# Eight small loads on ScalarE's queue, gate weights in halves, Pool's large memsets behind the first norm

## Chip, cores and metric

The kernel runs on one core of a Trainium2 chip. The time is device microseconds from the launch to the end on that core, as the median of several executions. The names of the engines are TensorE (PE in the profile, with its weight loads as PEld), VectorE (DVE), ScalarE (ACT), Pool (GpSimd) and SP (the engine that only issues transfers here).

## The reference

One decoder layer on 1024 tokens of width 1024, in float32. Cut to what matters:

```
h = x + W_out . concat(RMSNorm(StickBreakingAttention(q, k, v)), ConformerConv(c))
        with [q | k | v | c] = RMSNorm(x) . W_in          W_in: 1024 x 2560
y = h + PEER(RMSNorm(h))
PEER: per token 8 heads, each finds its 16 best of 16384 experts by two small key tables,
      act = gelu(u_tab[expert] . h),  y += gate * act * v_tab[expert]
```

The attention has 8 heads of 64 and is causal; the convolution group is a gated linear unit (`a * sigmoid(gate)`), a causal depthwise convolution of 31 taps, a layer norm and a swish. The expert rows (128 per token, from two tables of 64 MB) are gathered from device memory.

## The kernel before

The 1024 tokens are eight chunks of 128, one token per partition. `phase0` does norm, projection and, for the first chunk, everything else up to the list of experts; `phase1` gathers and adds expert rows for all chunks while it runs the front part of the next chunk beside it. This case touches only the begin of `phase0`.

For each chunk, ScalarE squares x (`square_x`, L664) and takes the root of the mean, VectorE scales (`norm_x`, L845 is the wide multiplication into `xn`), TensorE transposes `xn` (`transpose_x`, L492), ScalarE copies the result to `xnT` with the gains of the norm (`copy_xT`, L679), and TensorE multiplies by `w_in` in five banks of 512 columns (`project`, L514). The banks are A and G (the two halves of the gated linear unit), then Q, K, V, and lie in `w_sb`, 2 MB each. A float32 product of 128 x 512 appears as two records, so a bank is 16 records and a chunk 80.

The order on each queue is written out by hand, and semaphores join the queues:

- SP (L367 on) issues x of the first chunk, then the eight small vectors: five into `rows`, one partition per 128 numbers (L374), two head gains doubled by a broadcast (L377), and `conv_w` into `taps_row`, 31 partitions of 2 KB (L380). All eight add to one semaphore, `small_in`. Then it loads the banks of `w_in` (`load_w`, L386), the first bank A in two halves with a semaphore each, the others whole, with the x of the second chunk behind Q.
- Pool (L445 on) makes the identity and the mask, then fills `kT` and `vals` (each 128 x 4096) and the halo of `conv_in` with zeros (L458 to L460) and is then idle until the first list of experts.
- TensorE first waits for the identity and for all of `small_in`, and turns `rows` and `taps_row` (L474, L476). Only then come x's transposes and the projections.
- VectorE copies what was turned out of PSUM into `vec` and `taps` (L959, L960). `copy_xT` waits for both copies, since it needs the gains.
- ScalarE begins with a table load for the square root (L799), then `square_x(0)`.

The zeros are waited for by ScalarE only: before its first writes into `conv_in` (L730), `kT` (L719) and `vals` (L707).

Of the kernel before, what the change touches and what calls it, by code (L numbers as in the profile page):

```python
# [22 lines left out]
P = 128  # L23
SEQ, D = 1024, 1024
CHUNKS = SEQ // P
KT_D = D // P
HEADS, HD = 8, 64
AW = HEADS * HD
CW = D - AW
AB = AW // P  # L30
CB = CW // P
# [261 lines left out]
def phase0(block, nc, S, base, psum, ident, ident_b, mask, kT, vals, keys_T, w_kept, wo_sb, wq_sb, actT, qT,  # L293
# [5 lines left out]
    Q, K, V, A, G = range(GROUPS)  # L299
    ORDER = (A, G, Q, K, V)  # L300
# [10 lines left out]
    rows = m.tile("rows", [P, P], F32)  # L311
    taps_turn = Map(nc, m.at)
    taps_row = m.tile("taps_row", [TAPS, CW], F32)
# [22 lines left out]
    sem = nc.alloc_semaphore  # L336
# [13 lines left out]
    gated, glu_done = sem("gated"), sem("glu_done")  # L350
    qT_stored, hT_stored, h_kept = sem("qT_stored"), sem("hT_stored"), sem("h_kept")
    S.kT_copied, S.qT_stored, S.hT_stored = kT_copied, qT_stored, hT_stored
    w_second = sem("w_second")
    keys_in, keys_turned, keys_copied = sem("keys_in"), sem("keys_turned"), sem("keys_copied")
    NSMALL = 8
    LAST = CHUNKS - 1
# [10 lines left out]
    @block.sync  # L367
    def _(sp):
        sp.dma_start(x_in[:, :], x[0, 0:P, :]).then_inc(x_loaded, 16)

        r = 0
        for v, n in ((norm_mix_g, KT_D), (attn_out_g, AB), (conv_b, CB), (conv_ln_g, CB),
                     (conv_ln_b, CB)):
            sp.dma_start(rows[r:r + n, :], v[0, :].rearrange("(n p) -> n p", p=P)).then_inc(small_in, 16)  # L374
            r += n
        for v in (q_norm_g, k_norm_g):
            sp.dma_start(rows[r:r + 1, :].rearrange("o (two d) -> o two d", two=2),  # L377
                         v[0:1, :].unsqueeze(1).to_broadcast([1, 2, HD])).then_inc(small_in, 16)
            r += 1
        sp.dma_start(taps_row[:, :], conv_w[0, :, :]).then_inc(small_in, 16)  # L380
        def load_w(g):

            parts = 2 if g == ORDER[0] else 1
            for n in range(parts):
                k, rows_in = KT_D // parts, D // parts
                sp.dma_start(w_sb[:, ORDER.index(g), n * k:(n + 1) * k, :],  # L386
                             w_in[0, n * rows_in:(n + 1) * rows_in, g * BANK:(g + 1) * BANK]
                             .rearrange("(k p) n -> p k n", p=P)).then_inc(w_second if n else w_loaded[g], 16)

        def next_x(i):  # L390
            sp.wait_ge(x_normed, i + 1)
            sp.dma_start(x_in[:, :], x[0, bass.ds((i + 1) * P, P), :]).then_inc(x_loaded, 16)

        def store_q(i):
            sp.wait_ge(qT_copied, i + 1)
            sp.dma_start(qT_spill[bass.ds(i, 1), :, :].rearrange("o p n -> (o p) n"),
                         qT_out[:, :]).then_inc(qT_stored, 16)

        def store_h(i):
            sp.wait_ge(hT_copied, i + 1)  # L400
            sp.dma_start(hT_spill[:, :, bass.ds(i * P + HALO, P)], hT_out[:, :, :]).then_inc(hT_stored, 16)

        for g in (A, G, Q):
            load_w(g)
        next_x(0)
        for g in (K, V):
            load_w(g)
        for n, k in enumerate((peer_k1, peer_k2)):
            sp.dma_start(keys[:, :, n, :], k[0].rearrange("h n d -> n h d")).then_inc(keys_in, 16)
        store_h(0)  # L410
        sp.dma_start(w_kept[:, :, :], w_out[0].rearrange("(k p) n -> p k n", p=P)).then_inc(S.wo_loaded, 16)
        next_x(1)
        store_q(0)
        store_h(1)
        next_x(2)
        sp.wait_ge(keys_turned, 1)
        sp.dma_start(S.g_ffn[:, :], norm_ffn_g[0:1, :].to_broadcast([P, D])).then_inc(S.g_loaded, 16)
        sp.wait_ge(S.attended, HEADS)
        sp.dma_start(S.h_res[:, :], x[0, 0:P, :]).then_inc(S.x_in, 16)
        sp.wait_ge(S.tapped, TAPS * CB)  # L420
        sp.wait_ge(hT_stored, 32)
        sp.dma_start(conv_in[:, :, :], hT_spill[:, :, P:2 * P + HALO]).then_inc(S.c_in, 16)
        store_q(1)
        sp.wait_ge(qT_stored, 32)
        sp.dma_start(qT[:, :, :].rearrange("p b t -> p (b t)"), qT_spill[1]).then_inc(S.q_in, 16)
        sp.wait_ge(S.mixed, 1)
        for n, landed in enumerate((S.wq_first, S.wq_loaded)):
            at = slice(n * BANK, (n + 1) * BANK)
            sp.dma_start(w_kept[:, :, at], peer_wq[0, :, at].rearrange("(k p) n -> p k n", p=P)).then_inc(landed, 16)
        for i in range(2, CHUNKS):  # L430
            store_h(i)
            if i < LAST - 1:
                next_x(i + 1)
            if i == LAST:
                sp.wait_ge(projected[G], CHUNKS)
                sp.dma_start(wo_sb[:, :, :], w_out[0].rearrange("(k p) n -> p k n", p=P)).then_inc(S.wo_loaded, 16)
            store_q(i)
        sp.wait_ge(projected[K], CHUNKS)
        sp.dma_start(wq_sb[:, :, :], peer_wq[0].rearrange("(k p) n -> p k n", p=P)).then_inc(S.wq_loaded, 16)
        sp.wait_ge(qT_stored, 16 * CHUNKS)  # L440
        sp.wait_ge(hT_stored, 16 * CHUNKS)

    @block.gpsimd
    def _(pool):
        nc.gpsimd.memset(ident[:, :], 0.0).then_inc(zeroed, 1)  # L445
        nc.gpsimd.memset(mask[:, :], 0.0).then_inc(zeroed, 1)
        pool.wait_ge(zeroed, 2)
        nc.gpsimd.affine_select(out=ident[:, :], in_=ident[:, :], compare_op=ALU.not_equal, fill=1.0,
                                base=0, pattern=[[-1, P]], channel_multiplier=1).then_inc(consts, 1)

        nc.gpsimd.affine_select(out=mask[:, :], in_=mask[:, :], compare_op=ALU.is_gt, fill=NEG,
                                base=0, pattern=[[-1, P]], channel_multiplier=1).then_inc(consts, 1)
        nc.gpsimd.iota(counting[:, :, :], pattern=[[1, TOPK], [0, PH]], base=0, channel_multiplier=0,
                       allow_small_or_imprecise_dtypes=True).then_inc(consts, 1)
        pool.wait_ge(consts, 3)
        nc.gpsimd.tensor_copy(ident_b[:, :], ident[:, :]).then_inc(consts, 1)

        nc.gpsimd.memset(kT[:, :, :], 0.0).then_inc(zeroed, 1)  # L458
        nc.gpsimd.memset(vals[:, :, :], 0.0).then_inc(zeroed, 1)
        nc.gpsimd.memset(conv_in[:, :, 0:HALO], 0.0).then_inc(zeroed, 1)  # L460

        pool.wait_ge(S.experts_done, 1)
        for e in range(EARLY):
            if e >= EARLY_RING:
                pool.wait_ge(S.dotted, e - EARLY_RING + 1)
            nc.gpsimd.indirect_dma_start(  # L466
                w_kept[:, e % EARLY_RING, :], None, peer_u[0],
                bass.IndirectOffsetOnAxis(S.experts[0][:, e:e + 1], 0)).then_inc(S.early_in[e % EARLY_RING], 16)

    @block.tensor  # L470
    def _(pe):
# [25 lines left out]
        def project(i, g, half=None):  # L497
            if i == 0 and half != 1:
                pe.wait_ge(w_loaded[g], 16)
            if half != 1:  # L500

                if g == V:
                    pe.wait_ge(glu_done, i + 1)
                elif g == K:
                    pe.wait_ge(gated, i + 1)
                elif i:
                    pe.wait_ge(*{A: (v_copied, i), G: (kT_copied, i), Q: (qT_copied, i)}[g])
            n = KT_D // 2
            for k in {None: range(KT_D), 0: range(n), 1: range(n, KT_D)}[half]:
                if i == 0 and g == ORDER[0] and k == n:  # L510
                    pe.wait_ge(w_second, 16)
                if g == ORDER[0]:
                    pe.wait_ge(xT_copied, KT_D * i + k + 1)
                last = nc.tensor.matmul(ps[g], xnT[:, k, :], w_sb[:, ORDER.index(g), k, :],  # L514
                                        start=k == 0, stop=k == KT_D - 1)
            if half != 0:
                last.then_inc(projected[g], 1)
# [140 lines left out]
    def _(act):  # L658
# [119 lines left out]
        def chunk(i):  # L778
            if 3 <= i < LAST:
                square_x(i + 1)  # L780
                root_x(i + 1)
            gate(i)
            if i == 0:
                copy_glu(0)
                square_x(1)
                root_x(1)
            square_qk(i)
            root_qk(i)
            if i == 0:
                copy_qk(0)  # L790
            else:
                copy_glu(i)
            copy_v(i)
            if i < LAST:
                copy_xT(i + 1)
            if i:
                copy_qk(i)

        nc.scalar.preload_act_table(ACT.Sqrt)  # L799
        square_x(0)  # L800
# [1282 lines left out]
```

## Time and profile before

| | |
|---|---|
| runs | 2910.17, 2914.2 and 2912.07 us |
| median | 2912.07 us |
| span of the profiled execution, first to last instruction | 2910.3 us |
| another time of the profiled execution | none is given |
| TensorE busy | 89% of the span |
| VectorE, Pool, ScalarE busy | 73%, 68%, 30% |
| moved by DMA | 1125.04 MB, 387 GB/s on average |
| mean granted TensorE clock | 0.994 |

Times in the rows are microseconds from the begin of the span. In a timeline row stand the start, the duration, the engine, the line and what is written from what; a bracket at its end tells how long the engine had been idle and what ended that. A row of windows gives the stretch and its length, then busy time (and instructions) of PE, PEld, DVE, ACT and POOL, and last the granted clock, the busy share of the DMA engines and GB/s. "Q" behind an engine's name is its issuing of transfers. "Landing" is the time from the issue of a transfer until its semaphore has its full value. Busy shares are averages over stages with different limits, so a stretch has to be looked at by itself.

### The profile page before, as it was taken

What the parts mean: (1) busy time and instruction counts of PE and PEld (TensorE: products, weight loads), DVE (VectorE), ACT (ScalarE), POOL (GpSimd) and SP (SyncE); (2) the same over time, 40 slices, a digit from 0 to 9 for tenths busy, and PEclk for the clock granted to TensorE, in tenths of its full rate; (3) what the DMA queues carried; (4) which work ended last, traced back from release to release, by engine and by line L of the source; (5) the groups of instructions that cost most, each with busy time, mean ns of one, the idle gap of its engine ahead of it and who ended that gap; (6) DMA issues with size and microseconds to landing.
All of it is one profiled execution on the core that took longest, in us unless ns stands there. A gap on an engine that the chain in (4) does not pass through costs nothing.

```text
span 2910.3 us, 29785 instructions
## 1 busy us (share of the span) xinstructions
PE 2591.2 (89%) x7585; PEld 1173.6 (40%) x7585; DVE 2110.6 (73%) x5267; ACT 871.6 (30%) x2022; POOL 1986.1 (68%) x2061
## 2 busy tenths in 40 slices
PE   8999979889978899799979999799988999777777
PEld 4544434433523444244523444244523445222222
DVE  5789758866887678777887778777787757744444
ACT  3223232243213421253214521264214631211111
POOL 1026566677777777777777777777777777777775
PEclk9999999999999999999999999999999999999999
DMA  6239899899999999999999999999999999999999
GB/s 239 96 127 382 331 416 369 316 402 414 419 419 419 413 419 419 409 414 409 416 416 406 411 419 419 419 392 413 419 419 399 385 419 419 415 420 419 420 419 364
DMA packets 321344, 1125.04 MB, mean 387 GB/s; under 512 B 35937, under 2 KB 43641, under 8 KB 321176
## 3 DMA queue, kind: packets, MB, share of 16 engines
q0 software_dynamic: 294912, 1073.87, 91.7%
q1 hardware_dynamic: 26264, 49.27, 4.8%
q8 instruction: 63, 1.03, 0.1%
q14 instruction: 105, 0.86, 0.1%
HBM read 1114.62 MB, written 8.39 MB: 386 GB/s over the span
## 4 chain that ended last, share of the span: by engine, by line
PE 41%; DMA 25%; issue 16%; POOL 12%; DVE 4%; ACT 2%; POOLq 0%; SPq 0%; ACTq 0%; DVEq 0%
PE psum L1614 21%; DMA w_kept<-in_peer_u,experts 12%; DMA ring_v<-in_peer_v,experts 10%; PE psum L514 9%; POOL w_kept L1517 7%; POOL ring_v L1517 5%; PE psum L1038 3%; PE psum L1064 3%; PE psum L1548 2%; DVE w_kept L1933 1%; PE psum L1574 1%; DMA w_kept<-in_peer_v,experts 1%; PE psum L1564 1%; DMA qT_spill<-qT_out 1%; ACT L1751 0%
## 5 line engine op out<-in xcount | busy, mean ns | idle before, releaser
L1614 PE MATMUL psum<-ring_v,diag 128*128 128x512 f32 x3364 | 1619.6, 607 | 252.6 <-DMA ring_v<-in_peer_v,experts 163.9
L1933 DVE CUSTOM_DVE_ANT_0 w_kept<-w_kept,psum 128x1024 f32<-128x1024 f32 x928 | 1125.5, 1217 | 551.2 <-DMA w_kept<-in_peer_u,experts 548.1
L1517 POOL DMA_INDIRECT w_kept<-in_peer_u,experts x928 | 898.2, 968 | 300.1 <-issue 231.4
L1517 POOL DMA_INDIRECT ring_v<-in_peer_v,experts x878 | 847.8, 966 | 327.3 <-issue 234.5
L1614 PEld LDWEIGHTS psum<-ring_v,diag 128*128 128x128 f32 x3364 | 587.1, 191 | 1058.8 <-issue 775.2
L1760 ACT ACTIVATE diag<-ident,weights 128x128 f32<-128x128 f32 x981 | 354.2, 393 | 746.9 <-PE psum L1614 589.9
L1614 PE MATMUL psum<-w_kept,diag 128*128 128x512 f32 x560 | 269.9, 604 | 37.3 <-DMA w_kept<-in_peer_v,experts 23.5
L514 PE MATMUL psum<-w_sb,xnT 128*128 128x512 f32 x640 | 283.5, 599 | 0.8 <-ACT xnT L679 0.8
L466 POOL DMA_INDIRECT w_kept<-in_peer_u,experts x96 | 90.2, 940 | 236.7 <-DVE experts L1324 184.9
L1889 DVE SCALAR_TENSOR_TENSOR acc<-conv_in,taps,acc 128x128 f32<-128x128 f32 x720 | 205.0, 346 | 0.2
L514 PEld LDWEIGHTS psum<-w_sb,xnT 128*128 128x128 f32 x640 | 120.6, 192 | 143.4 <-issue 137.7
L1517 POOL DMA_INDIRECT w_kept<-in_peer_v,experts x146 | 141.2, 967 | 47.6 <-issue 39.0
L1614 PEld LDWEIGHTS psum<-w_kept,diag 128*128 128x128 f32 x560 | 97.1, 190 | 170.2 <-issue 155.2
L1064 PEld LDWEIGHTS psum<-actT,wq_sb 128*128 128x128 f32 x896 | 118.8, 191 | 57.0 <-issue 56.9
L1858 DVE TENSOR_TENSOR_SCAN log_keep<-log_keep,relu_z 128x256 f32<-128x256 f32 (+3 forms) x88 | 90.4, 1027 | 59.9 <-ACT log_keep L1693 59.7
L1064 PE MATMUL psum<-actT,wq_sb 128*128 128x128 f32 x896 | 119.5, 275 | 0.0
L1708 ACT ACTIVATE actT<-psum 128x256 f32<-128x256 f32 (+3 forms) x88 | 44.9, 510 | 242.8 <-PE psum L1564 242.8
L1038 PE MATMUL psum<-wo_sb,actT 128*128 128x512 f32 x224 | 113.2, 592 | 0.0
L952 DVE CUSTOM_DVE_ANT_0 w_kept<-w_kept,psum 128x1024 f32<-128x1024 f32 x96 | 110.5, 1215 | 0.3 <-DMA w_kept<-in_peer_u,experts 0.3
L1751 ACT ACTIVATE geld<-dots 128x16 f32<-128x16 f32 x64 | 13.3, 214 | 303.3 <-DVE dots L1933 303.0
L1548 PE MATMUL psum<-kT,qT 64*128 64x512 f32 (+3 forms) x176 | 84.0, 557 | 2.1 <-DVE relu_z L1860 1.1
L1574 PEld LDWEIGHTS psum<-vals,actT 128*128 128x128 f32 x560 | 71.7, 192 | 27.2 <-issue 26.8
(230 smaller groups left out, 1750.9 us busy)
## 6 DMA issues: line engine op xcount, KB each, us to landing
w_kept<-in_peer_u,experts POOLq DMA_INDIRECT x1024, 9.5
ring_v<-in_peer_v,experts POOLq DMA_INDIRECT x878, 9.5
w_sb<-in_w_in SPq DMA_DIRECT2D x4, 2048.0 KB, 17.6
x_in<-in_x SPq DMA_DIRECT2D x8, 512.0 KB, 6.3
w_kept<-in_w_out SPq DMA_DIRECT2D x1, 4096.0 KB, 14.8
h_res<-in_x SPq DMA_DIRECT2D x8, 512.0 KB, 6.8
w_kept<-in_peer_wq SPq DMA_DIRECT2D x2, 2048.0 KB, 10.6
wo_sb<-in_w_out SPq DMA_DIRECT2D x1, 4096.0 KB, 19.9
```

The costliest lines, as they stand in the source:

```text
L514: last = nc.tensor.matmul(ps[g], xnT[:, k, :], w_sb[:, ORDER.index(g), k, :], start=k == 0, stop=k == KT_D - 1)
L952: nc.vector.tensor_tensor_reduce(out=row, in0=row, in1=hn, scale=1.0, scalar=0.0, op0=ALU.mult, op1=ALU.add, accum_out=S.dots[:, e:e + 1]) ...
L1038: product = nc.tensor.matmul(z[0][:, j * BANK:(j + 1) * BANK], S.actT[:, k, :], wo_sb[:, k, j * BANK:(j + 1) * BANK], start=k == 0, stop=k ...
L1064: product = nc.tensor.matmul(z[0][:, h * P:(h + 1) * P], wq_sb[:, k, h * P:(h + 1) * P], S.actT[:, k, :], start=k == 0, stop=k == KT_D - 1)
L1517: nc.gpsimd.indirect_dma_start(slot(kind, n), None, peer_u[0] if kind == "u" else peer_v[0], bass.IndirectOffsetOnAxis(S.experts[c % 2][:, ...
L1548: last = nc.tensor.matmul(z, qT[lo:lo + HD, a // 2, :], kT[lo:lo + HD, a // 2, lo_key:hi_key], start=True, stop=not has_own)
L1574: last = nc.tensor.matmul(o_ps[:, a * HD:(a + 1) * HD], S.attT[:, b, :], vals[:, b, a * HD:(a + 1) * HD], start=n == 0, stop=n == len(orde ...
L1614: last = nc.tensor.matmul(y_ps[:, j * BANK:(j + 1) * BANK], diag[:, e % DIAGS, :], slot("v", n)[:, j * BANK:(j + 1) * BANK], start=e == 0, ...
L1760: nc.scalar.activation(diag[:, e % DIAGS, :], ident[:, :], ACT.Copy, scale=weights[:, e:e + 1]).then_inc(diagonal, 1)
L1858: nc.vector.tensor_tensor_scan(l[:, back], l[:, back], r[:, back], carry, ALU.add, ALU.add).then_inc(S.summed, counts(f))
L1889: nc.vector.scalar_tensor_tensor(out=acc[:, c, :], in0=conv_in[:, c, t:t + P], scalar=taps[:, c, t:t + 1], in1=acc[:, c, :], op0=ALU.mult, ...
L1933: nc.vector.tensor_tensor_reduce(out=row, in0=row, in1=hn, scale=1.0, scalar=0.0, op0=ALU.mult, op1=ALU.add, accum_out=dots[:, e:e + 1]).t ...
```

## The change

Three edits. ScalarE issues the eight small loads, ahead of its table load, so that SP goes from x straight to the weights. The bank G is loaded in two halves as A is, each with a semaphore, and TensorE waits for the second half in the middle of the bank. Pool waits for the first norm (`x_normed`) before it fills `kT`, `vals` and the halo.

```diff
--- before.py
+++ after.py
@@ -350,7 +350,8 @@
     gated, glu_done = sem("gated"), sem("glu_done")
     qT_stored, hT_stored, h_kept = sem("qT_stored"), sem("hT_stored"), sem("h_kept")
     S.kT_copied, S.qT_stored, S.hT_stored = kT_copied, qT_stored, hT_stored
-    w_second = sem("w_second")
+    HALVED = (A, G)
+    w_second = {g: sem(f"w_second{g}") for g in HALVED}
     keys_in, keys_turned, keys_copied = sem("keys_in"), sem("keys_turned"), sem("keys_copied")
     NSMALL = 8
     LAST = CHUNKS - 1
@@ -368,24 +369,14 @@
     def _(sp):
         sp.dma_start(x_in[:, :], x[0, 0:P, :]).then_inc(x_loaded, 16)
 
-        r = 0
-        for v, n in ((norm_mix_g, KT_D), (attn_out_g, AB), (conv_b, CB), (conv_ln_g, CB),
-                     (conv_ln_b, CB)):
-            sp.dma_start(rows[r:r + n, :], v[0, :].rearrange("(n p) -> n p", p=P)).then_inc(small_in, 16)
-            r += n
-        for v in (q_norm_g, k_norm_g):
-            sp.dma_start(rows[r:r + 1, :].rearrange("o (two d) -> o two d", two=2),
-                         v[0:1, :].unsqueeze(1).to_broadcast([1, 2, HD])).then_inc(small_in, 16)
-            r += 1
-        sp.dma_start(taps_row[:, :], conv_w[0, :, :]).then_inc(small_in, 16)
         def load_w(g):
 
-            parts = 2 if g == ORDER[0] else 1
+            parts = 2 if g in HALVED else 1
             for n in range(parts):
                 k, rows_in = KT_D // parts, D // parts
                 sp.dma_start(w_sb[:, ORDER.index(g), n * k:(n + 1) * k, :],
                              w_in[0, n * rows_in:(n + 1) * rows_in, g * BANK:(g + 1) * BANK]
-                             .rearrange("(k p) n -> p k n", p=P)).then_inc(w_second if n else w_loaded[g], 16)
+                             .rearrange("(k p) n -> p k n", p=P)).then_inc(w_second[g] if n else w_loaded[g], 16)
 
         def next_x(i):
             sp.wait_ge(x_normed, i + 1)
@@ -455,6 +446,7 @@
         pool.wait_ge(consts, 3)
         nc.gpsimd.tensor_copy(ident_b[:, :], ident[:, :]).then_inc(consts, 1)
 
+        pool.wait_ge(x_normed, 1)
         nc.gpsimd.memset(kT[:, :, :], 0.0).then_inc(zeroed, 1)
         nc.gpsimd.memset(vals[:, :, :], 0.0).then_inc(zeroed, 1)
         nc.gpsimd.memset(conv_in[:, :, 0:HALO], 0.0).then_inc(zeroed, 1)
@@ -507,8 +499,8 @@
                     pe.wait_ge(*{A: (v_copied, i), G: (kT_copied, i), Q: (qT_copied, i)}[g])
             n = KT_D // 2
             for k in {None: range(KT_D), 0: range(n), 1: range(n, KT_D)}[half]:
-                if i == 0 and g == ORDER[0] and k == n:
-                    pe.wait_ge(w_second, 16)
+                if i == 0 and g in HALVED and k == n:
+                    pe.wait_ge(w_second[g], 16)
                 if g == ORDER[0]:
                     pe.wait_ge(xT_copied, KT_D * i + k + 1)
                 last = nc.tensor.matmul(ps[g], xnT[:, k, :], w_sb[:, ORDER.index(g), k, :],
@@ -795,6 +787,17 @@
                 copy_xT(i + 1)
             if i:
                 copy_qk(i)
+
+        r = 0
+        for v, n in ((norm_mix_g, KT_D), (attn_out_g, AB), (conv_b, CB), (conv_ln_g, CB),
+                     (conv_ln_b, CB)):
+            act.dma_start(rows[r:r + n, :], v[0, :].rearrange("(n p) -> n p", p=P)).then_inc(small_in, 16)
+            r += n
+        for v in (q_norm_g, k_norm_g):
+            act.dma_start(rows[r:r + 1, :].rearrange("o (two d) -> o two d", two=2),
+                         v[0:1, :].unsqueeze(1).to_broadcast([1, 2, HD])).then_inc(small_in, 16)
+            r += 1
+        act.dma_start(taps_row[:, :], conv_w[0, :, :]).then_inc(small_in, 16)
 
         nc.scalar.preload_act_table(ACT.Sqrt)
         square_x(0)
```

## Rows read from the trace of the kernel before

**Rows 1.** Windows, long stretches: busy us per engine, granted clock, DMA share, GB/s
```profile
100.00:350.00 250.00, 248.50 (x788) 124.89 (x787) 214.57 (x588) 68.08 (x134) 93.05 (x99) 1.00 0.66 246
...
400.00:2900.00 2500.00, 2218.32 (x6433) 987.23 (x6432) 1814.72 (x4466) 748.05 (x1773) 1859.39 (x1924) 1.00 1.02 409
```

**Rows 2.** Timeline, SP's DMA issues at the begin: start us, us, what
```profile
1.20 0.37 SPq L374 DMA_DIRECT2D rows<-in_norm_mix_g  x1
...
2.92 0.73 SPq L377 DMA_DIRECT2D rows<-in_q_norm_g  x1
3.69 0.57 SPq L377 DMA_DIRECT2D rows<-in_k_norm_g  x1
4.31 0.41 SPq L380 DMA_DIRECT2D taps_row<-in_conv_w  x1
4.77 0.41 SPq L386 DMA_DIRECT2D w_sb<-in_w_in  x1
5.22 0.50 SPq L386 DMA_DIRECT2D w_sb<-in_w_in  x1
5.76 0.83 SPq L386 DMA_DIRECT2D w_sb<-in_w_in  x1
6.63 5.20 SPq L386 DMA_DIRECT2D w_sb<-in_w_in  x1
```

**Rows 3.** Timeline, ScalarE, VectorE and Pool in the first chunk: start us, us
```profile
0.74 1.28 ACT L799 ACT_TABLE_LOAD   x1 [0.74 <-PEq L2073]
...
4.10 1.06 ACT L664 ACTIVATE xn<-x_in 128x1024 f32<-128x1024 f32 x1 [2.08 <-DMA x_in<-in_x]
...
5.90 4.21 DVE L845 TENSOR_SCALAR xn<-x_in,x_stat 128x1024 f32<-128x1024 f32 x1
...
5.92 3.51 POOL L459 MEMSET vals<- 128x4096 f32 x1
...
11.01 0.18 DVE L959 COPY vec<-psum 128x26 f32<-128x26 f32 x1 [0.89 <-PE psum L476]
...
32.56 0.59 ACT L730 ACTIVATE conv_in<-psum 128x512 f32<-128x512 f32 x1
...
35.93 0.75 DVE L845 TENSOR_SCALAR xn<-x_in,x_stat 128x1024 f32<-128x1024 f32 x1
```

**Rows 4.** Chain of waits from the begin: start us, us, what
```profile
4.31 5.82 DMA taps_row<-in_conv_w
...
10.97 1.90 PE psum L492 x8
12.87 18.72 PE psum L514 x40
```

**Rows 5.** Timeline, TensorE's weight loads of the first projections
```profile
12.67 0.50 PEld L514 LDWEIGHTS psum<-w_sb,xnT 128*128 128x128 f32 x2 [0.20 <-DMA w_sb<-in_w_in]
...
20.80 0.19 PEld L514 LDWEIGHTS psum<-w_sb,xnT 128*128 128x128 f32 x1 [0.35 <-DMA w_sb<-in_w_in]
```

**Rows 6.** Tile w_sb, issues at 4.77, 5.76 and 6.63: time to landing
```profile
DMA to landing us min/median/max: 7.9/7.9/7.9
...
DMA to landing us min/median/max: 15.0/15.0/15.0
...
DMA to landing us min/median/max: 19.5/19.5/19.5
```

**Rows 7.** Windows, the first 21 us (columns as in rows 1)
```profile
1.00:4.00 3.00, 0.00 (x0) 0.00 (x0) 0.00 (x0) 1.02 (x1) 2.69 (x6) 1.00 0.51 179
4.00:5.00 1.00, 0.00 (x0) 0.00 (x0) 0.00 (x0) 0.90 (x1) 1.00 (x1) 1.00 0.00 1
5.00:6.00 1.00, 0.00 (x0) 0.00 (x0) 0.41 (x3) 0.45 (x3) 1.00 (x2) 1.00 0.26 21
6.00:10.00 4.00, 0.00 (x0) 0.00 (x0) 4.00 (x1) 0.00 (x0) 3.57 (x2) 1.00 0.97 302
12.70:20.80 8.10, 8.10 (x17) 3.58 (x16) 0.00 (x0) 2.88 (x8) 0.00 (x0) 1.00 1.05 387
```

## The prediction, made before the change was run

> **What bounds the kernel now.** I read the stretches of the whole span first, then the first 40 us in detail, since all three edits lie there. In the long stretch from 400 us on, the DMA engines are busy all the time [rows 1]: this is the gather of expert rows, and its length does not depend on how the kernel began. Before it, from 100 to 350 us, TensorE is busy 248.5 of 250 us [rows 1]. So a microsecond won or lost at the begin is handed on through a busy TensorE and then through a busy DMA, one for one, if it reaches TensorE's first projection at all. Nothing in these two stretches can multiply it. The question is thus when the first projection starts, and whether weights keep up with it afterwards.
>
> The begin, in the order of the chain of waits: SP issues x, then the eight small loads from 1.20 to 4.72, then weights [rows 2]. The chain goes from the last small issue, the convolution taps, over 5.82 us until they land at 10.13, then TensorE, which goes on without a break of weight until 31.59 [rows 4]. Beside it stands a second path that is ready at the same time: ScalarE squares x at 4.10, and VectorE's norm takes 5.90 to 10.11, 4.21 us for an operation that takes 0.75 us for the next chunk [rows 3]. Pool's memset of `vals` lies over it, 5.92 to 9.43 [rows 3]; 9.43 plus 0.75 is 10.18, so VectorE seems to have waited for the memset and then worked. A third path: the first half of A's weights lands at 4.77 + 7.9 = 12.67, exactly when the first projection's weight load begins, and that one waited 0.20 for it [rows 5, 6]. G's weights land at 5.76 + 15.0 = 20.76, and TensorE's first load of them is at 20.80 after a wait for that DMA [rows 5, 6]. So three things end within a few tenths of each other, and a gain needs all three to go.
>
> **The change, part by part.**
>
> *Pool.* The two large memsets and the halo move behind the first norm. That frees the norm: it costs 0.75 and not 4.21, 3.46 us. The memsets then run for 3.51 + 3.51 + 0.20 us from the norm's end (8.1, below) to about 15.3. Their first user is ScalarE's copy into `conv_in` at 32.56 [rows 3], 17 us later; without that cover it would cost the whole 7.2. What VectorE does meanwhile are the two copies of the small vectors out of PSUM at 11.0 [rows 3]; see the fourth case.
>
> *The small loads on ScalarE's queue.* I charge ScalarE what SP's issues took: 3.52 us, from 0.74 to 4.26, with the taps issued from 3.85 on and not from 4.31, 0.46 us earlier. Behind them on ScalarE stand its table load (1.28 [rows 3], until now hidden before x landed) and the square: it starts at 5.54 and not 4.10. The norm started 1.80 after the square did [rows 3], so now at 7.34, and ends at 8.09. That is 2.0 us earlier than now, although ScalarE is 1.4 us later. SP's weights start to be issued at 1.20, 3.57 us earlier. But x's 0.5 MB fills the DMA engines until about 4.0 (179 GB/s from 1 to 4), and weights moved only from about 6 on [rows 7], so the stream of weights wins some 2.2 us: A's first half 10.5 or sooner, no longer behind the taps, G's last byte 18.6, Q's 6.63 + 19.5 = 26.1 [rows 2, 6] becomes 23.9. TensorE takes 24 records from 20.80 to 31.59, or 7.2 us for 16, one bank of weights; a bank of 2 MB lands in 5.4 us at 387 GB/s [rows 4, 5, 7], so beyond Q weights never bind.
>
> *What the taps now meet.* The stream from 6 to 10 us is 302 GB/s, 1.21 MB [rows 7], enough for the taps and A's first half (1.11 MB); yet that half lands 2.54 us after the taps. A sixteenth of it, 65 KB, takes 2.7 us at 387/16 = 24 GB/s: one of the 16 DMA engines carries all 62 KB of the taps, and its share of A waits behind them. In the change the taps sit on another queue, and that engine has weights queued first (A and G issued from 1.20 to 3.1). Bounds for the landing of the taps: if they pass at once, 3.85 + 1.5 + 2.6 = 8.0 (1.5 for the first byte: issued at 4.31, nothing moves from 4 to 5 and little from 5 to 6 [rows 7]); if everything takes as long as now, 3.85 + 5.82 = 9.67; if in addition every packet of theirs waits for one of weights, 2.6 more, 12.3. Between 8.0 and 12.3 I take the middle, 10.15, which is where it stands now: the 0.46 us of earlier issue is eaten by sharing. The Trainium skill says in "DMA: Bandwidth & Descriptors", Queues, rings and completion order, that a DMA engine takes turns between its queues packet by packet; by that the upper half, 9.67 to 12.3, is the likely one, and the sum would be up to 2 us worse than mine. No row here shows two such queues at work.
>
> *G in halves.* One more issue on SP (0.4 us, hidden behind a full queue), one more wait on TensorE. G's first load waited 0.35, where its neighbours wait 0.24 for nothing but their turn; 0.1 us goes.
>
> *Sum.* Taps 0.0; the wait for A's first half −0.2; the wait for G −0.1; all else hidden. That is −0.3 us. The profiled execution spans 2910.3 us and gives no other time of its own; the median of the runs is 2912.07, 1.8 us above it, and I take that difference as it is: 2911.8.
>
> **The rivals.** A difference under 0.2% (5.8 us) is about what a measurement of this kernel cannot tell from no change.
>
> *The taps pass at once.* Landing at 8.0, x's transposes would start 0.84 us later as they do now (10.13 to 10.97 [rows 4]), at 8.84 (the norm is done at 8.09), and the projection 1.5 us after them (1.70 from 10.97 to 12.67, less the wait for weights), at about 10.4: −2.2 us, 2909.8. For it: 62 KB is little. Against it: that engine is behind all the others already now. More than this cannot come, since ScalarE's issues, table load and norm bound it at 8.09.
>
> *ScalarE's issues are held up behind SP's* (slower). SP's issue of Q took 5.20 us where A's halves took 0.4 to 0.5, and ended 0.8 us before A's first half landed [rows 2, 6]: a queue was full. With weights first, SP meets this at about 3.2 us, when ScalarE has issued up to `q_norm_g` (3.19) and has `k_norm_g` and the taps before it. If ScalarE can't issue while SP's issue stands, it goes on at 11.83 − 2.2 = 9.6: k's row, the taps at 10.25, landed between 14.3 (1.5 and 2.6 later) and 16.1 (5.82 as now), up to 18.7 with sharing. TensorE then starts 4.2 to 8.6 us late, minus 0.3; at 16.1 it is +5.6, 2917.7. It decides if SP's long issue begins before ScalarE's last. Against it: nothing in the rows says that the two share what is full. The Trainium skill, "Perfetto Trace Analysis", DMA Instruction — HWDGE, says that the unit which generates descriptors is locked for one issuer until all of them are generated, and that this is counted in the issue's time. By that rule this rival would be what happens; the trace has a single issuer of this kind, so no row can agree or disagree.
>
> *VectorE's two small copies wait for Pool's memsets* (slower). They come about 0.9 us behind the taps' landing, at 11.0, in the middle of the memsets (8.1 to 15.1). If they must wait as the norm did, ScalarE's `xnT` copies, which need them, are late by 0.6 (the end of `kT`) to 4.1 us (the end of `vals`); with 4.1, 2915.9. Against it: they read PSUM, the norm read SBUF. The Trainium skill, "SBUF — State Buffer", Who interferes with whom, gives the pair of ports that VectorE shares with Pool to certain two-port forms and to two SBUF inputs, which these are not. No row has such a copy beside a memset.
>
> **How the numbers follow.** Taps between 9.67 and 12.3, all else as in the sum: 0.50; its own range is 2911.3 to 2914. The taps pass at once: 0.28. ScalarE held: 0.16. Copies held: 0.06. To each comes the spread of the runs, 2910.17 to 2914.2. The range 2908.5 to 2917.0 holds the first two, the fourth, and the mild part of the third. Faster by over 0.2% needs 5.8 us, more than twice what the begin can give: 0.03. Slower by over 0.2% is half of the third case and a little besides: 0.08. Within: 0.89.
>
> **What would show it.** After the change: the norm of chunk 0 at 0.75 us, from about 7.3 (Pool's part). ScalarE's eight issues at 0.25 to 0.7 us each, ending near 4.3; one of several us would mean the third case. The landing of the taps, 5.8 to 8 us from their issue for the first case, 4.2 for the second. The first projection within 2 us of 12.67. The two PSUM copies at 0.2 and 0.3 us, 0.9 us behind the landing. TensorE's first load of G without a wait. The same distance from the first projection to the end of the span. The prediction is wrong if that distance changes by more than 2 us, so that the long gather stretch answers to how it was entered, or if the taps land past 12.3.

## The result and the profile after

The changed kernel takes 2916.24 us (median of 21 runs, 2915.35 to 2921.53), the kernel before 2912.68 us beside it (21 runs, 2909.99 to 2917.85). The ratio is 1.0014, with a 95% interval from 1.0008 to 1.0020: 4.1 us slower, between 2.3 and 5.8 (the two medians alone are 3.6 apart). That lies inside the range of the prediction, but it is a loss clear of the noise where 0.3 us of gain was forecast. A few single executions ran far longer, at a lower granted clock or without any sign of why (3079.53 us for the kernel before, 3053.02 and 5265.37 for one of the runs below), and no ratio counts them.

The timeline of the kernel after, with ScalarE's and SP's issues, the first norm and Pool's memsets (answers to [rows 2, 3]):

```profile
0.74 0.59 ACTq L794 DMA_DIRECT2D rows<-in_norm_mix_g  x1
...
3.56 0.57 ACTq L797 DMA_DIRECT2D rows<-in_k_norm_g  x1
4.17 0.48 ACTq L800 DMA_DIRECT2D taps_row<-in_conv_w  x1
4.67 1.28 ACT L802 ACT_TABLE_LOAD   x1 [4.67 <-issue]
5.97 1.06 ACT L656 ACTIVATE xn<-x_in 128x1024 f32<-128x1024 f32 x1
...
7.77 0.75 DVE L848 TENSOR_SCALAR xn<-x_in,x_stat 128x1024 f32<-128x1024 f32 x1
...
8.59 3.51 POOL L450 MEMSET kT<- 128x4096 f32 x1 [6.05 <-DVE xn L848]
12.03 3.51 POOL L451 MEMSET vals<- 128x4096 f32 x1
...
15.05 0.18 DVE L962 COPY vec<-psum 128x26 f32<-128x26 f32 x1 [6.53 <-PE psum L468]
```

All that the change was to do at once is there: the issues take 0.27 to 0.70 us each, the norm takes 0.75 and is done at 8.52 instead of 10.11, the memsets run behind it. But nobody uses the norm for six microseconds. The chain of waits of the kernel after tells why (answers to [rows 4]):

```profile
4.17 10.01 DMA taps_row<-in_conv_w
...
15.02 1.90 PE psum L484 x8
16.92 18.92 PE psum L506 x40
```

The taps, issued 0.14 us earlier than before, take 10.01 us to land instead of 5.82: at 14.18, 4.05 us later than before. TensorE's first weight load of the projection follows (answer to [rows 5]); it has no bracket, for the weights have long been there (A's first half landed 5.9 us after its issue at 1.19):

```profile
16.65 0.50 PEld L506 LDWEIGHTS psum<-w_sb,xnT 128*128 128x128 f32 x2
```

And the packets of the two queues tell what the taps met. One row for each queue, q1 being SP's and q10 ScalarE's, with packets, MB and share of the 16 DMA engines; the stretches are 6 to 8, 8 to 10 and 10 to 12 us of the kernel after, and in the last row 8.14 to 13.5 us, which holds the 31 packets of the taps and nothing else of ScalarE's:

```profile
q10 hardware_dynamic: 21, 0.00, 1.1%
...
q1 hardware_dynamic: 378, 0.74, 101.2%
q10 hardware_dynamic: 15, 0.02, 3.4%
...
q1 hardware_dynamic: 358, 0.71, 102.4%
q10 hardware_dynamic: 11, 0.02, 3.2%
...
q10 hardware_dynamic: 31, 0.06, 3.3%
```

The first packet of the taps starts at 8.15 and the last ends at 13.46, one every 174 ns. A DMA engine moves such a packet in some 85 ns (387 GB/s over 16 engines), so the taps get every second turn of one engine and weights get the other. Before 8.15 us nothing of the taps has moved at all: what the queue moves are the short rows, hardly any bytes. So the 10.01 us are 3.98 from the issue to the first packet, 5.32 of moving, and 0.72 from the last packet to the landing.

The loss is handed on whole through the first stage. This is ScalarE's last copy of q for the last chunk, in the kernel before and, below it, in the kernel after, 4.24 us later:

```profile
353.10 0.68 ACT L716 ACTIVATE qT_out<-psum,vec 128x512 f32<-128x512 f32 x1
```

```profile
357.34 0.68 ACT L708 ACTIVATE qT_out<-psum,vec 128x512 f32<-128x512 f32 x1
```

### The profile page after: what moved, and what is told of

It reads as the page before. It is cut to its first block, busy times and chain, and to the rows that moved or that the text cites. A ratio compares the mean times of both kernels' runs of the same rounds, so it can differ in the third digit from the quotient of the medians.

```text
span 2913.3 us, 29786 instructions
## 1 busy us (share of the span) xinstructions
PE 2599.4 (89%) x7585; PEld 1177.4 (40%) x7585; DVE 2107.2 (72%) x5267; ACT 871.0 (30%) x2022; POOL 1984.6 (68%) x2061
## 4 chain that ended last, share of the span: by engine, by line
PE 43%; DMA 20%; issue 17%; POOL 14%; DVE 4%; ACT 2%; POOLq 0%; ACTq 0%; DVEq 0%
PE psum L1617 22%; DMA ring_v<-in_peer_v,experts 12%; PE psum L506 9%; POOL w_kept L1520 8%; DMA w_kept<-in_peer_u,experts 6%; POOL ring_v L1520 5%; PE psum L1041 3%; PE psum L1067 3%; PE psum L1551 2%; DMA w_kept<-in_peer_v,experts 1%; PE psum L1577 1%; DVE w_kept L1936 1%; PE psum L1567 1%; DMA qT_spill<-qT_out 1%; PE psum L1085 0%
```

## The experiments

Each run is compared with the kernel before on the same chip. Three things are read from each: the start of the first projection's weight load (12.67 before, 16.65 after), the last copy of q (353.10 and 357.34), and the ratio. The ratios have intervals of 5 us and more, wider than most of the differences looked at here, so the readings rest on the profiles, one for each kernel.

| run | projection starts | last copy of q | median, us | ratio (95%) |
|---|---|---|---|---|
| Pool's edit alone | 12.57 | 352.83 | 2912.14 | 0.9996 (0.9987 to 1.0005) |
| small loads on ScalarE alone | 16.47 | 357.34 | 2915.77 | 1.0008 (0.9999 to 1.0017) |
| after, taps on SP | 12.23 | 351.92 | 2909.89 | 0.9991 (0.9982 to 1.0000) |
| after, taps in 30 + 1 rows | 11.87 | 352.53 | 2910.51 | 0.9990 (0.9981 to 0.9999) |
| after, weights held back | 14.23 | 353.73 | 2912.38 | 1.0002 (0.9993 to 1.0011) |
| before, taps in 30 + 1 rows | 11.87 | 352.19 | 2910.19 | 0.9994 (0.9985 to 1.0003) |
| the same and Pool's edit | 10.26 | 351.14 | 2908.36 | 0.9988 (0.9979 to 0.9998) |
| loads shared out | 8.86 | 348.24 | 2908.87 | 0.9988 (0.9979 to 0.9997) |
| after, taps first on ScalarE | 12.59 | 352.93 | see below | none |
| after, only taps on ScalarE | 10.28 | 350.05 | 2910.05 | 0.9992 (0.9982 to 1.0001) |

The first four went together, to part the three edits and the two properties of the taps' load (its queue, its 31 rows).

**Pool's edit alone.**

```diff
+        pool.wait_ge(x_normed, 1)
         nc.gpsimd.memset(kT[:, :, :], 0.0).then_inc(zeroed, 1)
```

> The kernel before with Pool's edit alone. Theory (the loss comes from the taps' transfer, which shares its one DMA engine with the weights on another queue): the first norm takes 0.75 us from 5.90 and ends at 6.65, the taps still land at 10.1 and the first projection still starts at 12.6 to 12.7; the ratio to the kernel before is 1.000 within 0.0006. Rival (Pool's late memsets cost, by VectorE's two copies or later): the copies into vec and taps take more than 0.3 us or start more than 1 us after the taps land, and the ratio is up to 1.0014.

The chain of waits and the timeline of this run:

```profile
4.30 5.74 DMA taps_row<-in_conv_w
```

```profile
5.74 0.75 DVE L846 TENSOR_SCALAR xn<-x_in,x_stat 128x1024 f32<-128x1024 f32 x1
6.55 3.51 POOL L459 MEMSET kT<- 128x4096 f32 x1 [4.02 <-DVE xn L846]
10.00 3.52 POOL L460 MEMSET vals<- 128x4096 f32 x1
10.92 0.19 DVE L960 COPY vec<-psum 128x26 f32<-128x26 f32 x1 [4.43 <-PE psum L477]
```

VectorE's copy out of PSUM starts in the middle of the second memset and takes 0.19 us, so it does not wait for it. The edit makes the norm 3.5 us shorter and moves nothing else: the taps bind as before. The rival with VectorE's copies falls.

**Small loads on ScalarE alone.** The diff's block of eight issues, moved to ScalarE's queue; Pool and `load_w` as before.

> The kernel before with the eight small loads on ScalarE's queue alone. Theory: the whole loss is here: the taps land at 14.2 within 0.5 us, the first projection starts at 16.5 to 16.9, the ratio is 1.0014 (1.0009 to 1.0019). The norm waits for Pool's memset as before but is hidden (ends at 10.2). Rival (the loss needs Pool's edit or G in halves): the taps land before 12 us and the ratio is under 1.0006.

The chain of waits:

```profile
4.17 9.83 DMA taps_row<-in_conv_w
```

The taps land at 14.00 and the last copy of q is at 357.34, the same hundredth as with all three edits. In the profile the whole loss is here. The ratio 1.0008 is lower than expected; its interval holds 1.0014, but 1.0000 too, so by itself it shows no loss.

**The taps on SP.**

```diff
         sp.dma_start(x_in[:, :], x[0, 0:P, :]).then_inc(x_loaded, 16)
+        sp.dma_start(taps_row[:, :], conv_w[0, :, :]).then_inc(small_in, 16)
...
-        act.dma_start(taps_row[:, :], conv_w[0, :, :]).then_inc(small_in, 16)
```

> The kernel after, but the taps (62 KB) are issued by SP between x and the weights, the other seven stay on ScalarE. Theory (the taps alternate packet by packet with weights on one DMA engine): on the same queue ahead of the weights they take their 2.6 us at full rate behind x and land before 8 us; what remains are the seven short rows, which in the kernel after were through at about 8 us; the projection starts at 10.7 to 11.5, the ratio to the kernel before is 0.9994 (0.9990 to 0.9998). Rival (any load on ScalarE's queue is slow by itself, or the seven rows are what is late): the projection starts later than 12.7 and the ratio is 1.000 or more.

The chain of waits:

```profile
3.53 6.22 DMA rows<-in_k_norm_g
...
12.50 18.02 PE psum L507 x40
```

The last landing comes at 9.75, 4.4 us earlier than in the kernel after. What is late now is a load of half a kilobyte, 6.22 us from its issue. I had expected the seven rows through at about 8, so I was 1.7 us off, and the start at 12.23 misses the 10.7 to 11.5: the short rows on this queue are slow too, whoever carries the taps. A part of it is the issue itself, which took 1.49 us here and 0.57 in the kernel after.

**The taps in 30 + 1 rows**, on ScalarE's queue as in the kernel after. `NSMALL` becomes 9.

```diff
-        act.dma_start(taps_row[:, :], conv_w[0, :, :]).then_inc(small_in, 16)
+        act.dma_start(taps_row[0:TAPS - 1, :], conv_w[0, 0:TAPS - 1, :]).then_inc(small_in, 16)
+        act.dma_start(taps_row[TAPS - 1:TAPS, :], conv_w[0, TAPS - 1:TAPS, :]).then_inc(small_in, 16)
```

> The kernel after, but the taps' load is cut into 30 rows and 1 row, both on ScalarE's queue. Theory (31 rows go to a single DMA engine, 30 rows can be spread over 15): the 30 rows are two packets for each engine and land within 1 us of their turn, so the last small load lands at 8.5 to 10 and the projection starts at 11 to 12.5, ratio 0.9994 to 1.0000. Rival (the number of DMA engines has nothing to do with it; the queue as a whole gets little): the last small load lands at 14 or later, ratio 1.0014.

The chain of waits:

```profile
4.70 4.70 DMA taps_row<-in_conv_w
```

And ScalarE's queue from 7.8 to 8.7 us (46 packets, of which 31 carry the taps' 0.06 MB):

```profile
q10 hardware_dynamic: 46, 0.06, 19.6%
```

One row less in the load, and the same bytes on the same queue beside the same weights land at 9.40 and not at 14.18. The first packet still starts only at 7.83, behind the short rows, but all 31 are through at 8.65, in 0.8 us instead of 5.3. It was not the queue's share of the DMA engines as a whole, but one engine that carried all 31 rows. The Trainium skill, "DMA: Bandwidth & Descriptors", section "Why a DMA increments its semaphore by 16 and not by 1" (its paragraph on how many engines), says that a load is spread over the largest number of engines up to 16 that divides the slowest dimension of both of its sides: by that 31 rows go to one, 30 to fifteen. This run agrees, with 0.8 us against 5.3.

The second four: is it the company of the weights, and how good does it get without the single engine?

**Weights held back.**

```diff
+        sp.wait_ge(small_in, 16 * NSMALL)
         for g in (A, G, Q):
             load_w(g)
```

> The kernel after, but SP waits for all eight small loads to land before it issues the first weights. Theory (the loads are slow because weights run on the same DMA engine): with nothing beside them ScalarE's eight loads land as SP's did before, the taps 4 to 6 us after their issue at 4.2, so at 8.2 to 10; weights then come late (issued from about 10), A's first half lands at 14 to 15 and binds the projection instead. Rival (ScalarE's queue is slow whatever runs beside it): the taps still land about 10 us after their issue, at 14.

The chain of waits:

```profile
4.04 4.97 DMA taps_row<-in_conv_w
9.03 5.16 DMA w_sb<-in_w_in
```

And ScalarE's queue from 5.1 to 8.7 us, the taps' 31 packets and one more:

```profile
q10 hardware_dynamic: 32, 0.06, 6.1%
```

Alone, ScalarE's eight loads are through at 9.01, and the taps take 4.97 us instead of 10.01. ScalarE's queue is not slow by itself; the weights beside it are what costs 5 us. The two parts can be told from the packets: the first one of the taps starts at 5.14, 1.1 us from the issue and not 4.0, and the last ends at 8.67, after 3.5 us and not 5.3. So the wait for the first packet is the larger part of the loss, 2.9 us, and the turns are the smaller, 1.8. A's first half then binds, at 14.19.

**The taps in 30 + 1 rows in the kernel before**: the same split with `sp.` for `act.`.

> The kernel before (all loads on SP, Pool as before), only the taps cut into 30 rows and 1 row. Theory (one DMA engine carried all 31 rows and its share of the weights stood behind them): the taps land before 7.5 us and A's first half before 10.5, instead of 10.1 and 12.7; the norm, which still waits for Pool's memset until 10.1, now binds alone: x's transposes start at 10.2, the projection at 11.9 to 12.2, ratio 0.9997 to 1.0000. Rival (the late landing has another cause): A's first half still lands at 12.7.

The chain of waits of this run begins with x and goes through the norm:

```profile
5.88 4.25 DVE xn L846
10.17 1.97 PE psum L493 x8
12.14 18.57 PE psum L515 x40
```

Now the chain holds no taps. TensorE has turned the vectors at 6.3, and the norm, which waits for Pool's memset, binds alone. A's first half no longer makes anybody wait at 11.87.

**Both.** The split and Pool's edit on the kernel before.

> As the last one, and Pool's edit with it. Theory: the norm ends at 6.6, the taps land before 7.5, and A's first half binds at 9.5 to 10.5, so the projection starts 2.2 to 3.1 us earlier than before; ratio 0.9990 to 0.9994. Rival (Pool's memsets behind the norm are not free): no earlier than the last one, ratio 0.9997 or more.

The chain of waits:

```profile
5.07 5.14 DMA w_sb<-in_w_in
10.26 19.38 PE psum L516 x40
```

A's first half lands at 10.21, 2.46 us earlier, with nothing queued before it on one engine, and binds. Here Pool's edit is worth 1.6 us of start, against 0.1 by itself: two limits that end together give nothing until both are gone. The ratio 0.9988 is 3.5 us faster, between 0.6 and 6.1.

**Loads shared out.** From the kernel after: SP issues `norm_mix_g`, `attn_out_g`, `conv_b`, `conv_ln_g` and the taps in 30 + 1 rows between x and the weights, ScalarE keeps three loads.

```diff
+        for v, n in ((norm_mix_g, KT_D), (attn_out_g, AB), (conv_b, CB), (conv_ln_g, CB)):
+            sp.dma_start(rows[r:r + n, :], v[0, :].rearrange("(n p) -> n p", p=P)).then_inc(small_in, 16)
+            r += n
...
+        act.dma_start(rows[20:24, :], conv_ln_b[0, :].rearrange("(n p) -> n p", p=P)).then_inc(small_in, 16)
```

> The kernel after (Pool's edit, G in halves), with the small loads shared out: SP issues four rows and the taps in 30 + 1 rows ahead of the weights, ScalarE only the last vector and the two head gains. Theory: weights begin right behind x and the taps, about 1.5 us earlier than in the kernel before, ScalarE's table load still ends before x lands, the norm ends at 6.7, A's first half lands at 8 to 9, and the projection starts at 8.5 to 9.5, ratio 0.9986 to 0.9990. Rival (short loads on ScalarE's queue are late whenever weights run): the last small load lands after 9 us and the projection starts at 11.5 or later.

The chain of waits:

```profile
3.67 5.14 DMA w_sb<-in_w_in
8.86 19.57 PE psum L513 x40
```

The first projection starts 3.81 us earlier than in the kernel before, when A's first half has landed at 8.81, and the last copy of q is 4.86 us earlier, the best of all. Some of the additional microsecond may be TensorE's clock. The stretch from 37 to 100 us, in the kernel before and, below it, in this run (the third figure from the end is the granted clock):

```profile
37.00:100.00 63.00, 61.30 (x206) 31.60 (x205) 52.41 (x167) 26.08 (x45) 0.00 (x0) 0.97 0.36 121
```

```profile
37.00:100.00 63.00, 61.29 (x216) 32.19 (x215) 53.97 (x172) 29.91 (x56) 0.00 (x0) 1.00 0.33 117
```

In the kernel before the granted clock is at the lower of its two levels, 1.2 and not 2.4 GHz, from about 56.6 for 3.4 us, with TensorE busy all through it and for six microseconds before; here it stays at 2.4. The run with weights held back stays at 2.4 too, and is the only other one that does. From the first projection to the last copy of q these two take 339.4 and 339.5 us, the kernel before 340.4. But no run changes the clock alone, and two others take 339.7 and 339.8 with the lower level in them, so how much of the microsecond is the clock's stays open. The rival of short loads that are late beside weights was not really asked: ScalarE's three loads moved before 4 us, and the first weights were issued at 3.67. Its ratio is again 0.9988 (0.9979 to 0.9997): a time better than both kernels, but not told apart from the simpler run above.

The last two ask where the taps' 10 us come from in the order of ScalarE's queue.

**The taps first on ScalarE's queue**, the seven rows behind; all else as after.

> The kernel after with the order on ScalarE's queue changed: the taps first, the seven rows behind. If the wait has two parts that add up (the 31 taps packets alternate with x and weights on one engine; each short load behind costs its own turn), the order changes nothing in the sum: the last small load lands at 12 to 14.2 and the projection starts at 14.5 to 16.7. If only the taps' packets were slow, the last small load lands as soon as they are through, at about 8.5 to 9, and the projection starts near 11.2.

The chain of waits:

```profile
4.33 5.78 DMA rows<-in_k_norm_g
...
12.86 18.58 PE psum L506 x40
```

The last small load lands at 10.11: between the two expectations, and neither holds as stated. The order matters by 4.1 us. Put first, the taps use the time from 2 us on, while ScalarE is still issuing the rows, and the rows come 2 us behind them; put last, they don't begin before 8.15. Of this kernel's runs only two count, 2911.84 (the profiled one) and 2913.75; two are too few for a ratio, and only the profile is used.

**Only the taps on ScalarE**, first thing; the seven rows on SP ahead of the weights.

> The kernel after with the taps alone on ScalarE's queue, first thing, and the seven rows back on SP ahead of the weights. Theory: the taps move beside x and in the gap before the weights start, land before 7, the norm ends at 6.7, and A's first half binds the projection at 9.5 to 10.5; ratio 0.9986 to 0.9993, as good as cutting the taps. Rival (a load of 31 rows on ScalarE's queue is late in any company): the taps land after 9 and the projection starts at 11.5 or later.

The chain of waits and the timeline:

```profile
3.73 4.08 DMA rows<-in_k_norm_g
...
10.55 18.08 PE psum L515 x40
```

```profile
5.93 1.06 ACT L665 ACTIVATE xn<-x_in 128x1024 f32<-128x1024 f32 x1 [3.36 <-DMA x_in<-in_x]
```

The projection starts at 10.28 as expected, but for another reason. A's first half landed at 9.9 and nobody waited for it; the chain goes through the last small load, which lands at 7.8. That is a short row on SP's queue; ScalarE's queue, and so the taps, moved nothing after 6.8. And x itself is late: its square starts at 5.93 where it did at 4.10, waiting for x. So the sharing works both ways: the big load that runs beside the taps has its share on the same engine, and lands when that share does. The norm ends at 8.5 and not at 6.7.

## Why the prediction was wrong

*The step that failed* is the landing of the taps, "Between 8.0 and 12.3 I take the middle, 10.15", which made the sum's term "Taps 0.0". It was 14.18, past the upper bound, and the term was 4.05. The bound of 12.3 was an issue at 3.85, 5.82 us as in the kernel before, of which 1.5 were to the first packet and 2.6 for 31 packets, and 2.6 more for waiting a turn for each. The turns were about right: moving took 5.32 us where those two terms give 5.2. The time to the first packet was not: 3.98 us and not 1.5, because the short rows ahead of the taps on ScalarE's queue were themselves moving among weights, until 8.1 us. I had charged the sharing to the taps' own packets alone, and nothing to the seven loads in front. (The issue came 0.32 us later than forecast, and the last packet landed in 0.7 us where the bound had 1.7 left.) The second mistake is the middle between the bounds, which charged the turns only in part and was a choice without a row behind it. A landing past 12.3 was named in advance as a sign that the prediction is wrong, and so it is. The Trainium skill's rule of turns in "DMA: Bandwidth & Descriptors", Queues, rings and completion order, which I named beside the choice and set aside, was on the right side: the 31 packets come one every 174 ns, and in 0.8 us when they are cut into 30 + 1 rows. In one thing the trace differs from that page, which puts several descriptors into one packet: here the turn changed after every 2 KB.

*Held up behind SP* (rival, 0.16): a start 4 us late was nearly its number too (4.2 to 8.6), but not its mechanism. In the kernel after, SP's issue of Q stands from 3.75 to 6.54, and ScalarE's issue of the taps falls into it:

```profile
3.75 2.79 SPq L377 DMA_DIRECT2D w_sb<-in_w_in  x1
```

The issue at 4.17 took 0.48 us, about as long as on SP before (0.41). So SP's long issue did not lock ScalarE out; the rule of the Trainium skill, "Perfetto Trace Analysis", DMA Instruction — HWDGE, as I applied it is not borne out here. The time was lost behind the issue, not in it. One issue of the other runs was longer: in the run with the taps on SP, `k_norm_g` took 1.49 us on ScalarE while SP's issue stood from 3.11 to 6.71. Even that one ended 1.7 us before SP's; what made it long stays open.

*The taps pass at once* (0.28): no. *Copies held by Pool's memsets* (0.06): no, the copy took 0.19 us beside a memset.

*Pool's edit*: right. The norm took 0.75 us and ended at 8.52 (forecast 8.09), because ScalarE's issues ended at 4.65, not 4.26. By itself it is worth 0.1 us of start.

*One engine of 16 carries the taps*: right. Worked out from the landings, it was shown by the cut into 30 + 1 rows, on either queue.

*G in halves*: no run has it alone, and nothing waited for G in the kernel after. With the first projection 4 us later, TensorE comes to G at about 24.9, 7 us after its second half landed at 17.8. The 0.1 us is gone as forecast, but for another reason.

*The stream of weights 2.2 us earlier*: it was more for A, whose first half landed at 7.1 against 12.67, and unused, since TensorE waited for the taps until 14.18.

*The distance from the first projection to the end stays*: up to 350 us it does, to 0.3 us (3.98 at the start, 4.24 at the last copy of q). In the gather the single runs spread by more than that: the two profiled executions end 3.0 us apart (2910.3 and 2913.3), the ratio says 4.1 with ± 1.8. Whether some of it comes back there stays open. In the other runs the last copy of q follows the start to within 1.1 us, and a part of that may be the clock, as said above: one for one is right to a microsecond and no closer.

*The bound of 0.2%*: the loss, 0.14%, stays under it, as the case with 0.89 said. But that a difference under 0.2% can't be told from no change was wrong: over 21 runs the interval is clear of 1.

What stays open too is why seven loads of 0.5 to 4 KB need until 8 us beside the weights. ScalarE's queue moves 16 packets from 4 to 6 us and 21 from 6 to 8. A single engine, at one turn every 174 ns, would move 11 in two microseconds, so this is few for loads of which most are spread over several; no run took one of them alone.

## What to carry to other kernels

A load issued earlier on a second queue need not land earlier if a large stream has been put beside it: ask for each small load how many DMA engines it is spread over, what else stands on those engines at that time, and what stands ahead of it on its own queue. The load of 31 rows was worth cutting (30 + 1) on either queue: whole, it was late by 4 to 5 us, and on SP's queue it made A's first half behind it late by 2.5. Other row counts without a large divisor up to 16 are worth a look for the same reason; only 31 was tried. Where three waits end within tenths of each other, time each edit beside the others' removal: Pool's edit was worth 0.1 us of start alone and 1.6 with the taps out of the way.

## What the runs showed of the hardware

Two queues that have packets for the same DMA engine took turns at it packet by packet: 2 KB packets of the second queue moved every 174 ns where one takes 85 ns. A large load waited for the engine that shares: the square of x started 1.8 us later with the taps beside x. A load of half a kilobyte took 6.22 us to land beside a stream of weights. VectorE's copies out of PSUM ran at 0.19 us beside a Pool memset, where the wide norm from SBUF to SBUF took 4.21 instead of 0.75. And an issue on ScalarE's queue took 0.48 us while SP's own issue stood for 2.79 us. The granted clock fell to half for 3.4 us at 53 to 61 us in ten of the twelve profiles, with TensorE busy before and in it (the kernel before), and not in the other two.
